# Attention logits of an fp32 kernel in two products per block instead of three: the rounded and the low part of the queries stacked in the rows of one stationary tile

## What is computed

```python
FOX_HEADS = 16
FOX_HEAD_DIM = 64
q = heads(q) * (FOX_HEAD_DIM ** -0.5)        # (1, 16, 512, 64)
k = heads(k)
logits = jnp.einsum('bhqd,bhkd->bhqk', qb, k).astype(jnp.float32)
logits = logits + cb[:, :, :, None] - c[:, :, None, :]
logits = jnp.where(q_pos[:, None] >= key_pos[None, :], logits, -jnp.inf)
p = jax.nn.softmax(logits, axis=-1).astype(v.dtype)
return jnp.einsum('bhqk,bhkd->bhqd', p, v)
```

## Time and profile before

| | before |
|---|---|
| median of 3 runs | 2255.65 us (2253.98 to 2257.08) |
| span of the profiled execution | 2253.8 us |
| TensorE (PE), matmuls | 2190.5 us, 97% |
| VectorE (DVE) | 1100.2 us, 49% |
| ScalarE (ACT) | 657.1 us, 29% |
| GpSimd (POOL) | 1499.1 us, 67% |
| mean granted clock of TensorE | 0.994 |

### The profile page before, as it was taken

How to read it: one execution, slowest core, us unless ns; L and a number is a source line. 1 busy time by engine, 2 the same in 40 slices (tenths; PEclk the granted TensorE clock), 3 DMA queues, 4 the chain that set the end, 5 groups by cost and what they waited for, 6 DMA issues and landing times.

```text
span 2253.8 us, 26917 instructions
## 1 busy us (share of the span) xinstructions
PE 2190.5 (97%) x9652; PEld 1717.7 (76%) x9652; DVE 1100.2 (49%) x1970; ACT 657.1 (29%) x1124; POOL 1499.1 (67%) x741
## 2 busy tenths in 40 slices
PE   7999999999999999999999999999999999999997
PEld 3877777868888886788767888887778777888886
DVE  6889974984433105666533222104877835222101
ACT  3322335132222104344332111103555534111100
POOL 5868575658777887444378777887332348877785
PEclk9999999999999999999999999999999999999999
DMA  6323223733322332122123332332222222323332
GB/s 249 102 76 94 84 75 121 274 110 101 94 94 93 100 101 80 66 76 75 47 75 103 93 93 93 103 102 85 66 66 66 66 66 76 94 94 96 98 103 84
DMA packets 56372, 216.00 MB, mean 96 GB/s; under 512 B 6216, under 2 KB 6216, under 8 KB 53088
## 3 DMA queue, kind: packets, MB, share of 16 engines
q1 hardware_dynamic: 52992, 206.96, 28.4%
q10 hardware_dynamic: 3296, 7.91, 1.0%
HBM read 212.70 MB, written 2.15 MB: 95 GB/s over the span
## 4 chain that ended last, share of the span: by engine, by line
PE 75%; DVE 12%; POOL 5%; issue 4%; ACT 2%; DMA 2%; SPq 0%; DVEq 0%; POOLq 0%; ACTq 0%
PE ps L370 59%; DVE y L1992 5%; POOL w_hi L955 2%; POOL w_lo L961 2%; DMA raw<-in_wstream 2%; PE ps L407 2%; PE ps L1298 1%; PE ps L597 1%; PE ps L1268 1%; PE ps L393 1%; PE ps L1173 1%; PE ps L397 1%; PE ps L394 1%; DVE qk L2003 1%; PE ps L1395 1%
## 5 line engine op out<-in xcount | busy, mean ns | idle before, releaser
L961 POOL TENSOR_TENSOR w_lo<-raw,w_hi 128x1024 fp32r<-128x1024 f32 x335 | 816.8, 2438 | 199.5 <-ACT w_hi L1835 175.6
L955 POOL TENSOR_TENSOR w_hi<-raw,ones 128x1024 fp32r<-128x1024 f32 x304 | 581.2, 1912 | 407.6 <-DMA raw<-in_wstream 407.1
L370 PE MATMUL ps<-u_hi,w_hi 128*128 128x512 f32 x1760 | 716.0, 407 | 6.5 <-DVE qk L2003 2.4
L370 PE MATMUL ps<-u_lo,w_hi 128*128 128x512 f32 x1760 | 695.5, 395 | 0.0
L370 PE MATMUL ps<-u_hi,w_lo 128*128 128x512 f32 x1760 | 695.3, 395 | 0.0
L370 PEld LDWEIGHTS ps<-u_hi,w_hi 128*128 128x128 f32 x1760 | 331.2, 188 | 85.9 <-issue 6.1
L370 PEld LDWEIGHTS ps<-u_hi,w_lo 128*128 128x128 f32 x1760 | 330.2, 188 | 80.5
L370 PEld LDWEIGHTS ps<-u_lo,w_hi 128*128 128x128 f32 x1760 | 330.9, 188 | 75.7 <-issue 3.6
L370 PE MATMUL ps<-f_hi,w_hi 128*128 128x512 f32 x528 | 208.6, 395 | 0.0
L370 PE MATMUL ps<-f_lo,w_hi 128*128 128x512 f32 x528 | 208.6, 395 | 0.0
L370 PE MATMUL ps<-f_hi,w_lo 128*128 128x512 f32 x528 | 208.6, 395 | 0.0
(11 more groups left out here) (360 smaller groups left out, 2938.5 us busy)
## 6 DMA issues: line engine op xcount, KB each, us to landing
raw<-in_wstream SPq DMA_DIRECT2D x342, 512.0 KB, 3.6
ada_buf<-in_ada SPq DMA_DIRECT2D x16, 1024.0 KB, 6.0
ada_start<-in_ada SPq DMA_DIRECT2D x8, 1024.0 KB, 16.9
cbc<-decay_rows ACTq DMA_DIRECT2D x7, 512.0 KB, 3.5
x<-in_xT SPq DMA_DIRECT2D x1, 2048.0 KB, 8.0
bc<-gate_rows ACTq DMA_DIRECT2D x4, 512.0 KB, 5.2
out_T<-x ACTq DMA_DIRECT2D x8, 256.0 KB, 2.2
prm<-in_params SPq DMA_DIRECT2D x1, 357.5 KB, 3.0
```

The source lines that it names most:

```text
L370: last = nc.tensor.matmul(out, a, b, start=(start and k == 0 and i == 0), stop=(stop and k == nk - 1 and i == 2))
L955: g.tensor_tensor(w_hi[slot][:], raw[slot][:], ones[:, 0:1].to_broadcast([P, D]), ALU.mult).then_inc(chunk_hi, 1)
L961: g.tensor_tensor(w_lo[slot][:], raw[slot][:], w_hi[slot][:].bitcast(f32), ALU.subtract).then_inc(chunk_split, 1)
```

## The change

The logits of a block are made by two products instead of three. The two parts of the queries of one head are stacked in one stationary tile, `q_both`: the rounded part in the head's own 64 rows and the low part in the other 64, where there were zeros. The rounded keys of each head are held twice, `k_twice`, in its own rows and in the other ones, so that one product gives hi x hi and lo x hi at once. The low part of the keys, `k_lo`, gets a tile for each head with zeros in the other rows, for the second product. So ScalarE rounds the keys in four passes over 64 rows, of which two write to the other half of the partitions, VectorE takes the keys' low part in two passes, and the queries' low part is written to the other half. The zeros are kept in four tiles instead of eight.

```diff
--- before.py
+++ after.py
@@ -215,8 +215,8 @@
     here[0] = phase_at
     a_hi = place("a_hi", KT * T, f32r, [KT, T])
     a_lo = place("a_lo", KT * T, f32r, [KT, T])
-    q_hi, q_lo, k_hi, k_lo = [[place(f"{n}{b}", T, f32r) for b in range(2)] for n in ("q_hi", "q_lo", "k_hi", "k_lo")]
-    q_hi, q_lo = [[(t[b], qz[2 * j + b]) for b in range(2)] for j, t in enumerate((q_hi, q_lo))]
+    q_both = [[place(f"q_both{b}{a}", T, f32r) for a in range(2)] for b in range(2)]
+    k_twice, k_lo = [[(place(f"{n}{b}", T, f32r), qz[2 * j + b]) for b in range(2)] for j, n in enumerate(("k_twice", "k_lo"))]
     fv = place("fv", T)
     va_hi = place("va_hi", 8 * P, f32r, [2, NT, P])
     va_lo = place("va_lo", 8 * P, f32r, [2, NT, P])
@@ -819,7 +819,7 @@
     v_ff = [Steps(ctx, nc, f"ff{i}_dve", ["sg", "sa", "f", "lo"], credit=2) for i in (2, 3)]
 
 
-    v_fg = Steps(ctx, nc, "fg_dve", ["one", "zero_q", "zero_hi", "zero_lo", "zs", "z0", "lf", "c", "zero_qz"])
+    v_fg = Steps(ctx, nc, "fg_dve", ["one", "zero_k", "zero_hi", "zero_lo", "zs", "z0", "lf", "c", "zero_kz"])
     a_fg = Steps(ctx, nc, "fg_act", ["abs", "exp", "ln", "cb0", "cb1"])
     p_fg = Steps(ctx, nc, "fg_pe", ["cb0", "cb1"])
     U = 2 * NT
@@ -1256,16 +1256,15 @@
 
             a, r = divmod(n, NT)
             qs, ks = slice(r * P, (r + 1) * P), slice(0, (r + 1) * P)
-            qh, ql, kh, kl = [t[i % 2] for t in (q_hi, q_lo, k_hi, k_lo)]
             if i == 0 and n == 0:
-                pe.wait_ge(v_fg.sem, v_fg.at("zero_qz"))
+                pe.wait_ge(v_fg.sem, v_fg.at("zero_kz"))
             if n == 0:
                 pe.wait_ge(v_qlow.sem, v_qlow.at("kl", i))
             if n >= 2 or i:
 
                 pe.wait_ge(v_N.sem, v_N.at(f"N{(n - 2) % U}", i if n >= 2 else i - 1))
-            for j, (l_, r_) in enumerate(tri(qh[a][:, qs], ql[a][:, qs], kh[:, ks], kl[:, ks])):
-                nc.tensor.matmul(ps[4 + n % 2][:, ks], l_, r_, start=(j == 0), stop=False)
+            for j, t in enumerate((k_twice, k_lo)):
+                nc.tensor.matmul(ps[4 + n % 2][:, ks], q_both[i % 2][a][:, qs], t[i % 2][a][:, ks], start=(j == 0), stop=False)
 
             p_L.did(nc.tensor.matmul(ps[4 + n % 2][:, qs], ident_b[:], late_b[:], start=False, stop=True), f"L{n}")
 
@@ -1688,9 +1687,14 @@
             if what == "q":
                 for a in range(2):
                     rows = slice(a * FOX_D, (a + 1) * FOX_D)
-                    ins = A(q_hi[i % 2][a][rows, :], ps[0][rows, :], ACT.Identity, scale=-float(FOX_D) ** -0.5)
+                    ins = A(q_both[i % 2][a][rows, :], ps[0][rows, :], ACT.Identity, scale=-float(FOX_D) ** -0.5)
+            elif what == "k":
+                for half in range(2):
+                    for a in range(2):
+                        o = (a + half) % 2
+                        ins = A(k_twice[i % 2][a][o * FOX_D:(o + 1) * FOX_D, :], ps[1][a * FOX_D:(a + 1) * FOX_D, :], ACT.Identity)
             else:
-                ins = A({"k": k_hi[i % 2], "v": fv}[what][:], ps[j][:], ACT.Identity)
+                ins = A(fv[:], ps[2][:], ACT.Identity)
             a_proj.did(ins, what)
 
         def fox_cbc(i):
@@ -2212,9 +2216,8 @@
 
             return V.memset(t[(1 - a) * FOX_D:(2 - a) * FOX_D, :].bitcast(f32), 0.0)
 
-        for t in (q_hi[0], q_lo[0], q_hi[1], q_lo[1]):
-            zeros(t[0], 0)
-        v_fg.did(zeros(q_lo[1][1], 1), "zero_q")
+        zeros(k_lo[0][0], 0)
+        v_fg.did(zeros(k_lo[1][0], 0), "zero_k")
         for t, step in ((va_hi, "zero_hi"), (va_lo, "zero_lo")):
             for a in range(2):
                 o = (1 - a) * FOX_D
@@ -2232,14 +2235,15 @@
         def fox_low(i, what):
 
             dve.wait_ge(a_proj.sem, a_proj.at(what[0], i))
-            if what == "ql":
-                for a in range(2):
-                    rows = slice(a * FOX_D, (a + 1) * FOX_D)
-                    ins = V.scalar_tensor_tensor(q_lo[i % 2][a][rows, :], ps[0][rows, :], -float(FOX_D) ** -0.5,
-                                                 q_hi[i % 2][a][rows, :].bitcast(f32), ALU.mult, ALU.subtract)
-                v_qlow.did(ins, "ql")
-            else:
-                v_qlow.did(V.tensor_tensor(k_lo[i % 2][:], ps[1][:], k_hi[i % 2][:].bitcast(f32), ALU.subtract), "kl")
+            for a in range(2):
+                rows, other = [slice(o * FOX_D, (o + 1) * FOX_D) for o in (a, 1 - a)]
+                if what == "ql":
+                    ins = V.scalar_tensor_tensor(q_both[i % 2][a][other, :], ps[0][rows, :], -float(FOX_D) ** -0.5,
+                                                 q_both[i % 2][a][rows, :].bitcast(f32), ALU.mult, ALU.subtract)
+                else:
+                    ins = V.tensor_tensor(k_lo[i % 2][a][rows, :], ps[1][rows, :], k_twice[i % 2][a][rows, :].bitcast(f32),
+                                          ALU.subtract)
+            v_qlow.did(ins, what)
 
         fox_scale(0, 0)
         fox_scale(0, 1)
@@ -2252,10 +2256,9 @@
         dve.wait_ge(v_fg.sem, v_fg.at("lf"))
         v_fg.did(V.tensor_tensor_scan(fc[R, :], one_row[R, :], ps[3][R, :], 0.0, ALU.mult, ALU.add), "c")
         fox_low(0, "kl")
-        zeros(q_hi[0][1], 1)
-        v_fg.did(zeros(q_lo[0][1], 1), "zero_qz")
+        zeros(k_lo[1][1], 1)
+        v_fg.did(zeros(k_lo[0][1], 1), "zero_kz")
         fox_scale(0, 2)
-        zeros(q_hi[1][1], 1)
 
         def fox_negated(i, n):
 
```

## The result

The changed kernel has a median of 2260.66 us over 20 runs (2256.82 to 2264.25), beside 2255.04 for 20 runs of the kernel before (2251.34 to 2259.44): a ratio of 1.002, with a 95% interval of 1.0013 to 1.0026. The forecast was 2257.1, its range 2250.7 to 2262. The measured median is 3.6 us above the forecast, near the upper end of the range. The profiled execution has a span of 2255.1 us, 1.3 more than the earlier trace rows; its own time, 2256.96, is nearly the lowest of the 20.

The account below looks back on a forecast made before the run. TensorE was taken to set the pace in turns 1 to 6. Terms +0.31 + 2.46 - 1.30 made +1.5 us, so the median goes from 2255.65 to 2257.1 us, range 2250.7 to 2262.

Parts of the forecast that it names:

- The removal: Third products of the logits left out, 64 in all: 1.30 us less a turn, 10.4 us over the stage.
- ScalarE's four passes and VectorE's two: Preparing the next pair's keys: rounding makes the chain 1.93 us longer, the low part 0.70, together 2.63.
- steady turn: Between first logits of successive pairs, 27.93 us before: new wait of 1.71 less 1.30 saved, +0.41 us, six times.
- (a): Key passes overlap like full tiles, so the chain grows by only 2.06 us: 2253.1 us; chance 0.20.
- (d): A key pass across the partition halves costs 0.70 us, adding 3.5 us in all: 2260.6 us; chance 0.12.
- The wait: TensorE stands still 1.71 us at the next pair's first logits, until the keys' low part is ready.
- pair 7: Last head pair, with no keys to prepare behind it: keeps its full saving, -1.30 us.
- (b): No new wait at the first logits, the keys are in time: -9.1 us, 2246.5 us; chance 0.10.
- Turn 0: First turn, up to pair 1's first logits, set by VectorE's and ScalarE's chain: +0.31 us.
- Turn 1: Second turn of the loop over head pairs, taken like the other steady turns: +0.41 us.
- the meeting of unit 5's division with GpSimd: VectorE's division, 0.67 us not 0.35, assumed to end with GpSimd's operation as before; if missed, 0.3 us less a turn.
- (c): TensorE's new standstills make the clock fall, two episodes of 3.4 us in turns 1 to 6: 2263.9 us; chance 0.08.

Follow-up runs that it names:

- the filled kernel: The changed kernel with six matmuls whose results nobody reads ahead of the wait for the keys' low part, in each pair but the first: 2258.74 us, ratio 1.0017.

## Why the forecast had the mechanism right and came out too low

- **The removal** was sized right: 1.26 us a turn in the kernel with two products and the old chain, against 1.30.
- **ScalarE's four passes and VectorE's two** cost what the queries' passes said, 2.43 us behind the first pass and 0.69 between the low parts. Writing to the other half of the partitions costs nothing more on ScalarE: in the steady turn the two passes that do (1038.08, 1038.68) are spaced like the two that don't. Rivals (a) and (d) fall. (The recorded (d) was priced too high in any case: only two of the four passes cross, so its 0.10 us more for each makes 0.2 in a chain and not 0.4.) The rule of the Trainium skill (ScalarE: Activation LUTs, "What ACT_TABLE_LOAD costs") that back-to-back ACTIVATEs overlap by about 93 ns doesn't hold for these 64-row passes, 0.60 apart at a duration of 0.59; for full tiles the trace comes near it with 0.11. Rival (a) stood on that overlap of full tiles.
- **The wait** came out at 1.60 us by the starts, and 28.36 - 26.68 = 1.68 by the turns with and without it; the forecast was 1.71. The steady turn changed by +0.43 (forecast +0.41), pair 7 by -1.19 (-1.30). Rival (b) is what the kernel with the second head's keys moved does, and the change itself does not.
- **Turn 0** was forecast at +0.31 and changed by 0.0 in the mean, give or take 1 us. The sum took one execution's turn 0 as the kernel's; that one, 29.76, was the longest of five.
- **Turn 1** is where a term was mis-sized: +1.04, not +0.41. The sum took all turns alike and put the meeting of unit 5's division with GpSimd at nothing, on the assumption that it "ends with that operation after the change as well". It does end with one everywhere. But where it lasts much as before in turns 2 to 6 (0.44 to 0.77 us in four executions, 0.35 to 0.81 in five before), in turn 1 it begins earlier beside the GpSimd operation and ends no sooner: 1.00 to 1.70 us against 0.35 to 0.72. The chain to the keys doesn't move forward with TensorE there, and the wait is 1.8 us in the trace's gap, not 1.4. About 0.2 us more is in the removal, worth 1.04 in turn 1 of the kernel with two products and the old chain (26.21 against 27.25) and not 1.26.
- **Rival (c)** was given 0.08 on the ground that the 3.3 us idle time at 1100.6 "were followed by no fall". That was one profile. The same idle time is followed by a fall in three of five, so it was no argument against (c). By the prediction's own sign, a granted clock under 1 between 930 and 1100, (c) came in part: one episode that cost 1.7 us, at the end of turn 1, in two of four executions, not two episodes of 3.4 in every one. That is 0.9 us of turn 2's +1.17 in the mean.
- **A slip without consequence:** three memsets fewer stand ahead of the stage (five became two), not two.

The profiled difference of +3.6 us is thus the forecast +1.5, less 0.3 for turn 0, with 0.6 for turn 1, 0.85 for the clock behind its wait, 0.1 for pair 7, and 0.8 in the parts that the change doesn't touch (+0.2 ahead, +0.6 behind). The last 0.8, and the 0.8 by which the mean of all runs differs more than the profiles do, I put down to chance in the clock's falls elsewhere: the one around 1577 to 1585 us is there in four of four after and three of five before. That is argued, not shown. So is what the new standstills have to do with the clock's share in the runs' +4.4: the filled kernel's gain is inside their spread, and the kernels with two products and no such standstill have the same mean clock. The first profile agreed with the forecast to 0.2 us partly by luck: its before had the longest turn 0, and its after had no fall in turn 2 or ahead of turn 7. That the range holds the measured median is partly luck too. Its upper end, 2262, was built from (d)'s price for crossing the halves and a new meeting with GpSimd in turn 0; the runs show the first as nothing, and the mean of turn 0 didn't rise. What filled that room is turn 1 and the clock.

## What to carry to other kernels

Fewer products pay in full only if the operands they need are still ready when the engine arrives: compare the added preparation with the slack of the wait it feeds, counted from where the waiting engine will then arrive. If it doesn't fit, sort the preparation by who is wanted first; here moving the second head's half out of the chain turned +4.4 us into 8.3 or 9.0 less than before. And take what varies by chance (a first turn, a clock that falls or not behind a given idle time) from several executions before it goes into a sum or argues against a rival.

## What the runs showed of the hardware

- VectorE's division of an fp32 tile stands until a GpSimd operation that runs has ended: 0.49 us became 2.29 for 128x512 (1035.09 to 1037.38, GpSimd's 1034.70 to 1037.09), 0.35 became up to 2.07 for 128x256. In the 14 profiles 308 of these divisions began beside a running GpSimd operation, and none ended before it: 241 were lengthened and ended 0.08 to 0.29 us behind it. The 588 that began beside none lasted 0.29 to 0.49 us, by their size. The Trainium skill (SBUF — State Buffer, "SBUF: two separate sides") has a lock of that kind on ports that the two engines share; the trace agrees.
- Two ScalarE or VectorE operations over 64 rows that take turns between the halves don't overlap (0.60 apart for 0.59, 0.69 apart for 0.67), where the one behind an operation over 128 rows starts 0.07 to 0.11 us before the end of the one ahead. For VectorE the Trainium skill (VectorE: DVE Perf Modes, "Two Vector instructions with no wait between them") says that an operation whose operand starts in another group of 32 partitions than the last one's begins only when the earlier ones have finished. The trace agrees, and ScalarE behaves alike. On VectorE the half is the cause and not the 64 rows. The queries' first low part starts 0.08 us before the end of the full tile ahead when it writes to rows 0 to 63 (kernel before, 1032.68), and 0.03 behind it when it writes to the other half (changed kernel, 1032.03). And behind the low part of head 0 alone, 64 rows too, the next operation starts at 1034.91, 0.07 before its end. On ScalarE each of these passes starts in another half than the one ahead, on its input or its output, so there no run tells this from a cost of the 64 rows.
- The granted clock falls from 2.4 to 1.2 GHz behind some idle times of TensorE and not behind others of the same length in the same program: two of four behind 1.8 us at the end of turn 1, six of nine behind 3.3 us ahead of turn 7 (and all five of the altered kernels, behind 3.3 to 3.7), none of twenty behind 1.2 to 1.6. The 3.4 us at the lower level in the row shown cost 1.7 us.
